# Block two of a two-block transformer kernel: norm factors applied to the products, attention woven into the following groups, the output turned per group

## The chip, the core and the metric

The kernel runs on one core of a Trainium2 chip. The metric is the device time of one execution in microseconds (us). The kernel before took 3091.04 us, the median of three runs (3089.74 to 3092.34). TensorE is called PE in the profile, VectorE DVE, ScalarE ACT, GpSimd POOL, SyncE SP.

## What is computed

Two blocks in f32 on one sequence of 256 tokens of width 2048. Block one (latent attention, short convolutions, a convolutional FFN) is not touched by the change, except that its last result now passes to block two in another way. Block two, with the last norm of block one, in the reference:

```python
x = rms_norm(x, g_final)                       # end of block one
hn = rms_norm_2(x, norm_mix_g)
z = hn @ w_in
q_a, k_a, v_a, q_b, k_b, v_b, f_logit, g_a, g_b = jnp.split(z, split_idx, axis=-1)
a = moba_attention(q_a, k_a, v_a)              # 8 heads of 128; with 256 tokens: causal, ALiBi slopes
bfx = forgetting_attention(q_b, k_b, v_b, f_logit, b_forget)   # 8 heads, causal, log-forget bias
merged = sigmoid(g_a) * (a @ w_proj_a) + sigmoid(g_b) * (bfx @ w_proj_b)
x = x + merged @ w_out
hm = rms_norm_2(x, norm_mlp_g)
x = x + square(relu(hm @ w_up)) @ w_down       # d_ff = 8192
return rms_norm_2(x, norm_final_g)
```

An rms norm multiplies each token by one number (the root factor) and each feature by a gain. The factor of a token passes through a product with weights unchanged, and through relu and square as its square.

## The kernel before

**Layout.** The activations stand turned, features on the partitions and tokens in the free dimension: `xt` holds 16 tiles (k = 0 to 15) of 128 features by 256 tokens. A product takes its weights in groups of 512 output columns. A group has 8 chunks of two k tiles (128 x 1024 f32, 512 KB); of `w_down` in block one the last groups have 6 chunks, of the projections 4. Every f32 operand of the large products is kept as two f32r parts, hi and lo, and each product is three matmuls (L1460, L1461, L1462: hi with hi, hi with lo, lo with hi), so a chunk is 24 matmuls of 128x256.

**Who does what.** SP loads raw chunks into a ring of eight (`raw`). ACT rounds a chunk to its hi part (`split`, L488), DVE subtracts to get the lo part (L818), into a ring of four (`whi`, `wlo`, NSPLIT = 4). So ACT and DVE can be four chunks ahead of PE, and split number n + 4 waits until PE has used chunk n. Each engine has its own program in a fixed order, tied to the others by semaphores. In `ahead(group, between, later)` ACT and DVE write the splits of the next group; before its fifth split stands `between`, the work on the result of the group that PE has just ended, and before its seventh `later`. PE writes groups in turn into the two halves of PSUM (`half0`, `half1`, four banks each), and `half_read` tells it that a half is free.

**Block two.** At the seam (`two_norms`, `norm_h2`) PE has ended the last `w_down` group; ACT squares `xt`, PE sums the squares over the partitions with a matrix of ones (`sums`, L1512: 16 f32 matmuls of 128x256), ACT takes the root (L532), DVE inverts (L882) and scales (L1254); the same again for `norm_mix_g_2`, whose result is split into `h2`. Then, for each branch (`alibi`, `fox`): two groups of q, two of k, two of v (token_product, L1490 to L1492), and all eight heads of attention at once, with q, k and v of eight heads in SBUF: scores (L1714, for fox with the bias matmuls L1718), maximum (L1293), exp (L634), scaling (L1106), transposes (L1725), weighted values (L1730, L1731). In the fox branch a small product FG (L1746 to L1748, 96 matmuls of 8 columns) makes the forget logits. Scores lie in the first half of PSUM and turned probabilities and results in the second, so no other group can run meanwhile. Then the eight gate groups, eight pairs of projections, `w_out`, the norm `norm_hm` (squares, sums, root, scaling, split, in one piece), four rounds of `w_up_2` and `w_down_2`, and the last norm followed by 32 transposes (L1778) to token rows, two copies (L1402) and two stores.

The line that makes attention wait for everything, and everything for attention, on PE:

```python
free(2)
attention(tag, score2(tag), turn2, weighted2)
pe.wait_ge(s_half_read, L.of("half_read", (tag, "done")))
```

Of the kernel before, what the change touches and what calls it, by code (L numbers as in the profile page):

```python
# [54 lines left out]
def constants():  # L55
# [19 lines left out]
    c["dist"] = blocks(np.where(q >= k, q - k, FAR))  # L75
    c["causal"] = blocks(np.where(q >= k, 0.0, -FAR))
# [92 lines left out]
def program(nc, ins, consts, out, known, traced):  # L169
    with ExitStack() as ctx:  # L170
# [53 lines left out]
        s_lfw = sem("lfw")  # L224

# [6 lines left out]
        def folded(h):  # L232
            return h[:, 0:2, :].rearrange("p b (s t) -> p (b s) t", s=2)

# [20 lines left out]
        eps = sb("eps", [P, 1])  # L255

# [49 lines left out]
        sc = ExitStack()  # L306
        heads2 = [sb(f"heads2_{i}", [P, HEADS, 2 * T], F32R, scope=sc) for i in range(2)]
        h2 = sb("h2", [P, KT, 2 * T], F32R, scope=sc)
        sc2 = ExitStack()
        q2 = sb("q2", [P, HEADS, T], scope=sc2)  # L310
        k2 = sb("k2", [P, HEADS, T], scope=sc2)
        v2 = sb("v2", [P, TB, HEADS * P], scope=sc2)
        dist = sb("dist_sb", [P, TB, T], scope=sc2)
        causal = sb("causal_sb", [P, TB, T], scope=sc2)
        upto = sb("upto_sb", [P, TB, T], scope=sc2)
        after = sb("after_sb", [P, TB, T], scope=sc2)
        sc2.close()
        sc2 = ExitStack()
        sigs = [sb(f"sig{i}", [P, KT, T], scope=sc2) for i in range(2)]
# [3 lines left out]
        outrow = sb("outrow", [P, TB, D], scope=sc)  # L323
        sc.close()

        p2 = sq[:, 0, :].rearrange("p (a b t) -> p a b t", a=2, b=2)
        pt2 = sq[:, 1, :].rearrange("p (a b t) -> p a b t", a=2, b=2)
        lfw = tmp[:, :, :].rearrange("p (a b) t -> p a b t", a=2)
        conv_y = [sq[:, i, :].rearrange("p (b t) -> p b t", b=4) for i in range(2)]
# [18 lines left out]
        def _(sp):  # L348
# [80 lines left out]
            groups("w_in_2", 6)  # L429

            sp.wait_ge(s_act_lo, L.of("act_lo", ("h2", KT - 1)))
            for t, n in ((dist, "dist"), (causal, "causal"), (upto, "upto"), (after, "after")):
                sp.dma_start(t[:], consts[n].rearrange("p (a t) -> p a t", a=TB)).then_inc(s_mask_in, 16)
            groups("w_in_2", 6, 3072)
            load(W["w_in_2"], 0, KT, F_AT, 8)
            with L.loop(4) as i:
                group("w_in_2", i * GW + GA_AT)
                group("w_in_2", i * GW + GB_AT)
            with L.loop(4) as i:
# [3 lines left out]
            for f in range(5):  # L443
                if f < 4:
                    groups("w_up_2", 4, f * D)
                if f > 0:
                    groups("w_down_2", 4, 0, (f - 1) * HT)
# [30 lines left out]
        def _(act):  # L478
# [322 lines left out]
            for g in range(3):  # L801
                ahead(STD, turn)
# [1011 lines left out]
```

## Time and profile before

| | us |
|---|---|
| Median of three runs | 3091.04 |
| The profiled execution, its own time | 3089.91 |
| Its span, first to last instruction | 3088.1 |
| PE busy / PE weight loads busy | 2825.3 (91%) / 2681.3 (87%) |
| DVE busy | 1823.5 (59%) |
| ACT busy | 1213.8 (39%) |
| Mean granted TensorE clock | 0.94 of full |
| Share of PE in the chain that ended last | 84% |

The share of busy time is an average over the whole program. What counts is where PE stands still, and at which clock it runs: clock 1.00 is 2.4 GHz and 0.50 is 1.2 GHz. A row of the timeline gives the start, the duration, the instruction, and in brackets how long the engine had been idle and what ended that.

### The profile page before, as it was taken

The numbers are of one execution on the slowest core, as the hardware profiler recorded it, in microseconds if no ns is written. First come the engines' busy times: TensorE is split into PE (matmuls) and PEld (weight loads), VectorE is DVE, ScalarE is ACT, GpSimd is POOL, SyncE is SP. The second block draws the span as 40 slices with busy tenths as digits, with TensorE's granted clock in tenths as the row PEclk, the third lists the DMA queues.
The fourth block names the chain that finished last, engine by engine and source line by source line (L and its number), as shares of the span: only waits on it lengthen the run. The fifth ranks groups of instructions, "written<-read, shape, count | busy, mean of one in ns | idle before, by whom it ended". The sixth has DMA issues, their size and how long they took to land.

```text
span 3088.1 us, 53349 instructions
## 1 busy us (share of the span) xinstructions
PE 2825.3 (91%) x21436; PEld 2681.3 (87%) x21436; DVE 1823.5 (59%) x2109; ACT 1213.8 (39%) x1370; POOL 17.6 (1%) x24
## 2 busy tenths in 40 slices
PE   5879977778999999999798997999899999999998
PEld 4579963468999999999795885999898999999997
DVE  3979965687666665665544443445645554555544
ACT  3733321234554453443433332444334443433332
POOL 0000000000000000000000001000000000000000
PEclk9989986789999999999998896999999999999999
DMA  5959943446655656565364450565454656566552
GB/s 176 385 165 331 327 144 95 150 160 223 198 184 177 197 185 187 160 211 178 108 186 128 130 171 28 150 181 186 163 184 131 189 185 187 187 184 187 187 185 75
DMA packets 288373, 551.55 MB, mean 179 GB/s; under 512 B 19386, under 2 KB 28328, under 8 KB 287464
## 3 DMA queue, kind: packets, MB, share of 16 engines
q1 hardware_dynamic: 286984, 547.18, 55.6%
q10 hardware_dynamic: 1248, 2.42, 0.2%
q8 instruction: 97, 1.59, 0.2%
q14 instruction: 44, 0.36, 0.0%
HBM read 547.43 MB, written 2.10 MB: 178 GB/s over the span
## 4 chain that ended last, share of the span: by engine, by line
PE 84%; DVE 10%; ACT 2%; issue 2%; DMA 1%; ACTq 1%; DVEq 0%; POOL 0%; SPq 0%
PE half L1460 24%; PE half L1461 24%; PE half L1462 24%; DVE wlo L818 3%; PE half L1512 2%; PE half L1490 1%; PE half L1491 1%; PE half L1492 1%; DVE acc L840 1%; DVE acc L837 1%; DVE tmp L1138 1%; PE half L1661 1%; PE half L1650 1%; PE half L1651 1%; PE half L1730 1%
## 5 line engine op out<-in xcount | busy, mean ns | idle before, releaser
L818 DVE TENSOR_TENSOR wlo<-raw,whi 128x1024 fp32r<-128x1024 f32 (+2 forms) x917 | 1095.9, 1209 | 891.6 <-ACT whi L488 889.9
L488 ACT ACTIVATE whi<-raw 128x1024 fp32r<-128x1024 f32 (+2 forms) x917 | 950.2, 1047 | 1277.0 <-PE half L1462 1111.2
L1460 PE MATMUL half<-hf,whi 128*128 128x256 f32 x2400 | 673.4, 281 | 10.9 <-DVE hf L891 5.1
L1461 PE MATMUL half<-hf,whi 128*128 128x256 f32 x2400 | 672.4, 280 | 0.0
L1462 PE MATMUL half<-hf,wlo 128*128 128x256 f32 x2400 | 671.4, 280 | 0.0
L1460 PE MATMUL half<-h,whi 128*128 128x256 f32 x1776 | 503.6, 284 | 37.6 <-issue 15.9
L1461 PE MATMUL half<-h,whi 128*128 128x256 f32 x1776 | 501.6, 282 | 0.0
L1462 PE MATMUL half<-h,wlo 128*128 128x256 f32 x1776 | 501.0, 282 | 0.0
L1461 PE MATMUL half<-hid,whi 128*128 128x256 f32 x1712 | 478.7, 280 | 0.0
L1462 PE MATMUL half<-hid,wlo 128*128 128x256 f32 x1712 | 478.1, 279 | 0.0
L1460 PE MATMUL half<-hid,whi 128*128 128x256 f32 x1712 | 477.9, 279 | 0.0
L1460 PEld LDWEIGHTS half<-hf,whi 128*128 128x128 f32 x2400 | 452.8, 189 | 11.9 <-issue 10.9
L1462 PEld LDWEIGHTS half<-hf,wlo 128*128 128x128 f32 x2400 | 452.1, 188 | 0.0
L1461 PEld LDWEIGHTS half<-hf,whi 128*128 128x128 f32 x2400 | 451.6, 188 | 0.0
L1460 PEld LDWEIGHTS half<-h,whi 128*128 128x128 f32 x1776 | 339.4, 191 | 39.0 <-issue 33.7
L1462 PEld LDWEIGHTS half<-h,wlo 128*128 128x128 f32 x1776 | 339.0, 191 | 0.0
L1461 PEld LDWEIGHTS half<-h,whi 128*128 128x128 f32 x1776 | 338.8, 191 | 0.0
L1460 PEld LDWEIGHTS half<-hid,whi 128*128 128x128 f32 x1712 | 321.4, 188 | 0.0
L1461 PEld LDWEIGHTS half<-hid,whi 128*128 128x128 f32 x1712 | 321.3, 188 | 0.0
L1462 PEld LDWEIGHTS half<-hid,wlo 128*128 128x128 f32 x1712 | 320.7, 187 | 0.0
L1512 PE MATMUL half<-sq,ones 128*128 128x256 f32 (+1 forms) x236 | 68.2, 457 | 38.4 <-ACT sq L526 38.4
L1460 PE MATMUL half<-mix,whi 128*128 128x256 f32 x256 | 74.6, 291 | 29.9 <-DVE tmp L1138 17.4
(216 smaller groups left out, 2863.2 us busy)
## 6 DMA issues: line engine op xcount, KB each, us to landing
raw<-in_w_up SPq DMA_DIRECT2D x288, 512.0 KB, 4.0
raw<-in_w_in SPq DMA_DIRECT2D x216, 512.0 KB, 3.8
raw<-in_w_down SPq DMA_DIRECT2D x212, 512.0 KB, 4.7
raw<-in_w_ada SPq DMA_DIRECT2D x192, 512.0 KB, 5.9
raw<-in_w_out SPq DMA_DIRECT2D x64, 512.0 KB, 4.7
raw<-in_w_proj_a SPq DMA_DIRECT2D x16, 512.0 KB, 4.5
raw<-in_w_proj_b SPq DMA_DIRECT2D x16, 512.0 KB, 4.7
raw<-in_w_up SPq DMA_DIRECT2D x16, 384.0 KB, 3.3
```

The lines of the kernel that those rows point to most:

```text
L488: A(whi[:, s, 0:elems], raw[:, c, 0:elems], ACT.Copy).then_inc(s_hi_ready, 1)
L818: V.tensor_tensor(wlo[:, s, 0:elems], raw[:, c, 0:elems], whi[:, s, 0:elems].bitcast(F32), ALU.subtract).then_inc(s_drained, 1)
L837: V.scalar_tensor_tensor(a, w[:, 0, :], s[:, 0:1], a, ALU.mult, ALU.add).then_inc(s_dve_step, 1)
L840: V.scalar_tensor_tensor(a, w[:, 1, :], s[:, 1:2], a, ALU.mult, ALU.add).then_inc(s_drained, 1)
L1138: ins_ = V.reciprocal(flat(tmp), flat(tmp))
L1460: mm(o, hi, x[:, 0:T], start=(k == 0 and b % 2 == 0), stop=False, skip_group_check=True)
L1461: mm(o, hi, x[:, T:2 * T], start=False, stop=False, skip_group_check=True)
L1462: return mm(o, lo, x[:, 0:T], start=False, stop=(k == nk - 1), skip_group_check=True)
L1490: mm(o, xh, hi, start=(k == 0), stop=False)
L1491: mm(o, xh, lo, start=False, stop=False)
L1492: ins_ = mm(o, xl, hi, start=False, stop=(k == nk - 1))
L1512: ins_ = mm(half()[:, 0, 0:width], ones[:], sq[:, j % 2, b * width:(b + 1) * width], start=(c + b == 0), stop=(c == chunks - 1 and b == pe ...
```

## The change

- **Norm factors behind the products.** `h2` and `hf` are made of `xt` with the gain alone, per group of four tiles, right behind each group that finishes these tiles (`round_x`, `lo_x`, `square_x`). The sums of squares are taken by PE one group later (`add_squares`), into an own PSUM bank. DVE turns the two norms at the seam into one factor (`roots`), and multiplies it in where q, k, v and gates leave PSUM (`times`, `values`, `gates`). For the MLP the squared factor (`root_squared`) is multiplied in behind `w_down` (`scaled_onto_x`).
- **Attention woven in.** A set `s` is now four heads: a group of q, of k, of v. The six steps of its attention are handed to PE behind chunks 1, 4 and 7 of the next two groups (`side` in `product`), to ACT and DVE at the like places of `ahead`. Scores, turned probabilities, results and sums have four PSUM banks of their own; the groups use the other four.
- **Merging.** `merged` is an own buffer, waited for per group; gates are scaled and projections gated in the instruction that leaves PSUM.
- **Output per group.** The last norm's gain is multiplied in by rows, its factor as a scale of the finished rows; squares are summed by ACT's accumulator. The transposes of groups 0 to 2 stand in the products of groups 1 to 3. Four stores take the place of two.
- The order of the groups is q, k, v, q, k, v, FG, and q, k, v twice more; loops of block two from `w_in_2` to the projections are written out.

The diff, cut to what the prediction speaks of:

```diff
+        score_bank, turn_bank, head_bank, sum_bank = [halves[i // 2][:, 2 + i % 2, :] for i in range(4)]
...
-                ahead(DN11 if g < 3 else STD, turn if g < 3 else two_norms)
+            def into_second(g):
+                turn()
+                if g == 0:
+                    act.wait_ge(s_columns, L.of("columns", "ggm"))
+                round_x("h2", g, h2, lambda k: ggm[:, k:k + 1])
+                square_x(g)
+                square_x(g, lambda k: col("g_final", k))
...
+            for s in range(4):
+                before = att[s - 1] if s > 0 else None
+                side = [{} if before is None else d for d in ({6: before}, {1: before, 4: before, 6: before}, {1: before, 4: before})]
+                ahead(STD, turn, side={2: roots()} if s == 0 else side[1])
+                ahead(STD, turn, side=side[2])
...
             for g in range(3):
-                ahead(STD, turn)
+                ahead(STD, turn, (lambda: rows(g - 1)) if g > 0 else None)
+            rows(2)
             turn()
-            squares(flat(xt))
-            root(T, rstd[:, 0:T], D)
+            rows(3)
+            act.wait_ge(s_normed, L.of("normed", "out"))
+            A(rtok[:, 2:4], rtok[:, 2:4], ACT.Sqrt).then_inc(s_root, 1)
...
+            def roots():
+                dve.wait_ge(s_summed, L.of("summed", ("sq", L.n["squared"] - 1)))
+                step(V.tensor_scalar(r1, sum_bank[:, 0:T], 1.0 / D, EPS, ALU.mult, ALU.add))
+                step(V.reciprocal(r1, r1))
+                step(V.scalar_tensor_tensor(rr, sum_bank[:, T:2 * T], 1.0 / D, r1, ALU.mult, ALU.mult))
+                step(V.tensor_scalar(rr, rr, EPS, None, ALU.add))
+                step(V.reciprocal(rr, rr))
+                tt(rr, rr, r1, ALU.mult).then_inc(s_normed, 1)
...
+            def scaled_onto_x(t, key=None):
+                times(tmp[:], r5[:])
                 dve.wait_ge(s_half_read, L.at("half_read"))
-                V.scalar_tensor_tensor(conv_y[1], conv_y[0], 0.0, conv_y[0], ALU.max, ALU.mult).then_inc(s_batch, 1)
...
+                x4 = xt[:, bass.ds(t, 4), :]
+                tt(x4, tmp[:], x4).then_inc(s_stored_x, 1)
...
                     if last:
                         ins_.then_inc(s_chunk_used, 1)
...
                         L.add("hi_ready")
+                        if side and k // KC in side:
+                            next(side[k // KC], None)
...
+            def attend(tag, s):
+                heads = range(4 * (s % 2), 4 * (s % 2) + 4)
+                pe.wait_ge(s_half_read, L.of("half_read", ("k", s)))
+                for j in range(6):
+                    if j < 4:
+                        h = heads[j]
...
+                        score2(tag, h, s).then_inc(s_scores, 1)
...
+                    if 0 < j < 5:
+                        g = heads[j - 1]
+                        for qb in range(TB):
+                            pe.wait_ge(s_probs, L.of("probs", (tag, g, qb)))
+                        turn2(g).then_inc(s_pt_turned, 1)
...
+                    if j > 1:
+                        g = heads[j - 2]
...
+                        weighted2(g).then_inc(s_heads, 1)
...
+                    yield
...
+            for s in range(4):
+                side = {} if s == 0 else {n: att[s - 1] for n in (1, 4, 7)}
+                product(of(h2), ready="h2" if s == 0 else None, side={5: add_squares(2, False, True)} if s == 0 else side)
+                product(of(h2), side={7: token_roots()} if s == 0 else side)
                 token_product(h2)
...
-            pe.wait_ge(s_act_lo, L.of("act_lo", "merged"))
-            groups(4, h2)
-            sums()
+            for g in range(4):
+                product(of(merged), ready="merged" if g == 0 else None, side={5: add_squares(1, g == 1, False)} if g > 0 else None)
...
+            for g in range(4):
+                product(of(hid[1]), side={5: turn_out(g - 1)} if g > 0 else None)
+            for _ in turn_out(3):
+                pass
```

How the instructions stand. **First place:** PE, the start of attention. Before, right behind the last v group (L1492); `half0<-k2,q2` are scores, `half1<-ident_sb,sq` transposes of probabilities, `half1<-sq,v2` the weighted values:

```order
L1492 MATMUL half0<-whi,h2 128x512
L1714 MATMUL half0<-k2,q2 128x128 [waits half_read]
L1714 MATMUL half0<-k2,q2 128x256
L1714 MATMUL half0<-k2,q2 128x128
L1714 MATMUL half0<-k2,q2 128x256
L1725 MATMUL half1<-ident_sb,sq 128x128 [waits probs] x2
L1725 MATMUL half1<-ident_sb,sq 128x128
L1730 MATMUL half1<-sq,v2 128x256 [waits pt_copied]
L1731 MATMUL half1<-sq,v2 128x128
L1714 MATMUL half0<-k2,q2 128x128
```

With the change, the third step of the first set, between the q group and the k group of the next set (L1627 to L1629 are the matmuls of a product):

```order
L1629 MATMUL half0<-h2,wlo 128x256
L1899 MATMUL half0<-k2,q2 128x128 [waits maxed]
L1899 MATMUL half0<-k2,q2 128x256
L1909 MATMUL half0<-ident_sb,sq 128x128 [waits probs]
L1909 MATMUL half0<-ident_sb,sq 128x128 x2
L1914 MATMUL half1<-sq,v2 128x256 [waits pt_copied,half_read]
L1915 MATMUL half1<-sq,v2 128x128
L1627 MATMUL half1<-h2,whi 128x256 [waits drained,half_read]
```

A head's score, the transposes of the head before it and the values of the head before that now stand together, with two or three chunks of a product between two such steps.

**Second place:** DVE, the same step. `wlo<-raw,whi` is the lo part of a weight chunk, `q2<-half0,rq` takes q out of PSUM with the factor. With the change:

```order
L909 TENSOR_TENSOR wlo<-raw,whi 128x1024 [waits hi_ready] x3
L960 TENSOR_TENSOR q2<-half0,rq 128x1024 [waits chunk_used]
L1418 SCALAR_TENSOR_TENSOR sq<-dist_sb,half0 128x384 [waits scores]
L1423 TENSOR_REDUCE stat<-sq 128x1 [waits dve_step]
L1423 TENSOR_REDUCE stat<-sq 128x1
L960 TENSOR_TENSOR heads2_0<-half1,heads2_0 128x256 [waits rounded]
L1197 RECIPROCAL stat<-stat 128x1 [waits expd]
L1201 TENSOR_SCALAR sq<-sq,stat 128x128 [waits dve_step]
L1197 RECIPROCAL stat<-stat 128x1 [waits expd]
L1201 TENSOR_SCALAR sq<-sq,stat 128x256 [waits dve_step]
L909 TENSOR_TENSOR wlo<-raw,whi 128x1024 [waits hi_ready] x2
```

Before, no `wlo` stood between the first and the last instruction of an attention; now the splits that PE needs next are queued behind each step.

## Rows read from the trace of the kernel before

**Rows 1.** Page part 2, busy tenths and granted TensorE clock in 40 slices.
```profile
PE   5879977778999999999798997999899999999998
PEclk9989986789999999999998896999999999999999
```

**Rows 2.** Timeline of PE, end of block one: start, duration, instruction, [idle before <-releaser].
```profile
1496.68 8.99 PE L1512 MATMUL half<-sq,ones 128*128 128x256 f32 x32 [5.22 <-ACT sq L526]
...
1524.62 0.58 PE L1460 MATMUL half<-h,whi 128*128 128x256 f32 x1 [4.98 <-DVE h L865]
```

**Rows 3.** Timeline of PE around the two attention stretches.
```profile
1665.22 2.90 PE L1714 MATMUL half<-k,q 128*128 128x128 f32 x8 [3.69 <-DVE v L1305]
...
1713.02 0.57 PE L1460 MATMUL half<-h,whi 128*128 128x256 f32 x1 [1.36 <-DVE stat L1300]
...
1867.10 0.35 PE L1748 MATMUL half<-whi,h 128*128 128x8 f32 x1
...
1937.45 0.58 PE L1460 MATMUL half<-h,whi 128*128 128x256 f32 x1 [1.36 <-DVE stat L1300]
```

**Rows 4.** Timeline of PE before the w_out and the w_up products.
```profile
2219.38 0.57 PE L1460 MATMUL half<-h,whi 128*128 128x256 f32 x1 [8.84 <-DVE h L865]
...
2316.97 10.14 PE L1512 MATMUL half<-sq,ones 128*128 128x256 f32 x32 [4.78 <-ACT sq L526]
...
2332.09 0.58 PE L1460 MATMUL half<-hf,whi 128*128 128x256 f32 x1 [4.98 <-DVE hf L865]
```

**Rows 5.** Chain of waits at the end: start, us, what.
```profile
3058.07 1.24 DVE xt L865
...
3081.48 2.29 DVE outrow L1402
```

**Rows 6.** Windows: us; PE, PEld, DVE, ACT, POOL busy (count); clock, DMA, GB/s.
```profile
1713.00:1721.00 8.00, 7.98 (x45) 7.99 (x46) 1.22 (x1) 1.06 (x1) 0.00 (x0) 0.63 0.01 2
1856.00:1862.00 6.00, 6.00 (x30) 6.00 (x30) 0.00 (x0) 0.00 (x0) 0.00 (x0) 0.50 0.68 228
1937.00:1941.00 4.00, 3.55 (x17) 3.56 (x18) 0.07 (x2) 0.00 (x0) 0.00 (x0) 0.53 0.00 0
2080.00:2120.00 40.00, 40.00 (x342) 40.00 (x341) 19.43 (x16) 16.27 (x16) 0.00 (x0) 1.00 0.59 185
2219.00:2227.00 8.00, 7.62 (x47) 7.63 (x48) 1.25 (x2) 1.06 (x1) 0.00 (x0) 0.68 0.01 2
2332.00:2340.00 8.00, 7.91 (x49) 7.92 (x50) 8.00 (x23) 4.60 (x11) 0.00 (x0) 0.71 0.00 0
```

**Rows 7.** Chain of waits inside the forgetting attention, at clock 0.50.
```profile
1885.37 0.85 PE half L1714 x2
...
1889.23 0.46 PE half L1725 x2
```

**Rows 8.** Line L1512, instructions of 3064 to 3068.9 us: min/median/max ns.
```profile
L1512 PE MATMUL half<-sq,ones x25: 379/379/424, 3063.6 to 3068.9; 128*128 128x256 f32 x25
```

**Rows 9.** Timeline of PE, four small f32 matmuls inside a block-one product.
```profile
702.64 0.95 PE L1431 MATMUL half<-ones,acc 128*128 128x1 f32 x8
703.45 0.36 PE L1460 MATMUL half<-mix,whi 128*128 128x256 f32 x1
```

**Rows 10.** Groups of DVE and ACT, 1600 to 3088.1 us: busy, mean ns, idle.
```profile
L818 DVE TENSOR_TENSOR wlo<-raw,whi 128x1024 fp32r<-128x1024 f32 x452 | 548.5, 1222 | 596.7 <-ACT whi L488 596.7
...
L488 ACT ACTIVATE whi<-raw 128x1024 fp32r<-128x1024 f32 x452 | 475.1, 1057 | 694.1 <-PE half L1462 621.6 <-PE half L1492 56.4 <-PE half L1748 15.2
```

**Rows 11.** Timeline of DVE, the seam: onto xt, and a reciprocal of the norm.
```profile
1493.80 1.65 DVE L1179 SCALAR_TENSOR_TENSOR xt<-half,mod_f,xt 128x256 f32<-128x256 f32 x4
...
1506.22 1.75 DVE L882 RECIPROCAL rstd<-rstd 128x256 f32<-128x256 f32 x1 [10.77 <-ACT rstd L532]
```

**Rows 12.** Timeline of ACT, a table load and its user.
```profile
1870.47 1.28 ACT L760 ACT_TABLE_LOAD   x1
1871.76 0.22 ACT L760 ACTIVATE lf<-lf 128x16 f32<-128x16 f32 x1
```

More of the change, by code:

```diff
@@ L490, in split, with ahead @@
                 L.add("drained")
-            def ahead(group, between=None, later=None, sums=0):
+            def ahead(group, between=None, later=None, sums=0, side=None):
                 L.end = L.n.get("hi_ready", 0)
@@ L505, in ahead @@
                     between()
+                if len(chunks) <= 4 and side and 4 in side:
+                    next(side[4], None)
                 if len(chunks) <= 6 and later:
@@ L842, in sum_chunks, with ahead @@
                     L.add("mod_chunks")
-            def ahead(group, between=None, later=None, sums=0):
+            def ahead(group, between=None, later=None, sums=0, side=None):
                 L.end = L.n.get("hi_ready", 0)
@@ L857, in ahead @@
                     between()
+                if len(chunks) <= 4 and side and 4 in side:
+                    next(side[4], None)
                 if len(chunks) <= 6 and later:
@@ L1375, in _ @@
-            for g in range(4):
-                ahead(STD, lambda: (onto_x(4 * g), norm_hm() if g == 3 else None))
-            def squared_relu(buf, t, key=None):
-                taken(conv_y[0])
+                lo_batch(merged, 4 * i, 4, ("merged", i))
+            for i in range(4):
+                first = i == 0
+                ahead(STD, lambda: gate(sig_a), side={1: att[3], 4: att[3], 6: att[3]} if first else None)
+                ahead(PRJ, lambda: gate(sig_b[:]), side={1: att[3], 4: att[3]} if first else None)
+                ahead(PRJ, branch_a)
+                ahead(STD, lambda: branch_b(i))
@@ L1733, in _, with add_squares @@
-            for branch, tag in enumerate(("alibi", "fox")):
-                with L.loop(2):
-                    for _ in range(2):
-                        product(of(h2), ready="h2" if branch == 0 else None)
+            def add_squares(count, first, last):
+                for i in range(count):
+                    n = L.n["squared"]
+                    pe.wait_ge(s_squared, L.of("squared", n))
+                    for b in range(4):
+                        ins_ = mm(sum_bank[:, i * T:(i + 1) * T], ones[:], sq[:, n % 2, b * T:(b + 1) * T],
+                                  start=(first and i + b == 0), stop=(last and b == 3), skip_group_check=True)
+                    ins_.then_inc(s_summed, 1)
+                    L.mark("summed", ("sq", n))
+                    L.add("squared")
+                yield
```

556 lines of the change are left out of this document (346 added, 210 removed).

## Prediction

> **What bounds the kernel now.** I read the page first: PE is busy 91% of the span and holds 84% of the chain that ended last. The 40 slices then show where it is not at its work: from the end of block one on (slice 20 of 40), PE is at 9 except in slices 20, 22, 25, 29 and 40, and the clock at 9 except in 22, 23 and 25, the two attentions [rows 1]; a gap that two slices share does not show at this grain. So DVE and ACT, at 59% and 39%, do not bound it on average; the dense stretches do, at 342 matmuls in 40 us, 0.117 us each and 2.8 us a chunk [rows 6], and the gaps between them. Next I read the timeline of PE for the edges of each gap, then the windows for the slow clock behind it. A gap costs its length, and after it the products run for some microseconds at 1.2 GHz: of 7.98 us behind the first attention, 45 matmuls are worth 45 x 0.117 = 5.3 us, so 2.7 us are lost; likewise 1.6 us behind the second, 2.1 us behind the third gap and 2.2 us behind the fourth [rows 6]. The six stretches, each with that loss:
>
> A, the seam: PE idles from 1496.68 - 5.22 = 1491.46 and the first `h2` matmul starts at 1524.62 [rows 2]: 33.2, and 1.5 for the clock (taken as behind the second attention): 34.7 us.
> B, attention alibi: from 1665.22 - 3.69 = 1661.53 to 1713.02 [rows 3]: 51.5 + 2.7 = 54.2 us.
> C, attention fox: from the end of FG at 1867.45 to 1937.45 [rows 3]: 70.0 + 1.6 = 71.6 us.
> D, waiting for the merged input: 8.8 + 2.1 = 10.9 us [rows 4, 6].
> E, the MLP norm: from 2316.97 - 4.78 = 2312.19 to 2332.09 [rows 4]: 19.9 + 2.2 = 22.1 us.
> F, the tail: from 3058.05 (DVE starts at 3058.07 [rows 5]) to the end of the span at 3088.1: 30.1 us.
> Together 223.6 us in which PE makes no product of block two. The change takes all six apart; what counts is what must be put in the dense stream instead.
>
> **What comes in their place on PE.**
> Sums of squares: 12 chunks of four f32 matmuls of 256 columns, 32 at the seam and 16 at the MLP; the last norm's 16 are gone. At full clock 25 records start within 5.3 us, 0.22 each, two to a matmul [rows 8]: 48 x 0.44 = 21.2 us.
> Attention: at clock 0.50 a score matmul of 256 columns takes 0.85 us and two transposes 0.46 [rows 7]; at full clock I take half. An alibi head has 384 columns of scores (0.64), three transposes (0.35) and 384 columns of values (0.64): 1.63 us. A fox head has 640 columns more, 2.70 us. Eight of each: 34.6 us.
> Going in and out of the product stream: four tiny f32 matmuls inside a product took 0.81 us for eight records, and behind them one start came 0.08 us late [rows 9]. For waits on several semaphores I take 0.15 us a time, for 24 attention steps and 12 other insertions: 5.4 us.
> The transposes of three of the four output groups, 24 at 0.12: 2.8 us.
> Clock behind FG: FG keeps PE busy with matmuls of 8 columns, and the clock is 0.50 in it all the same [rows 6]. FG stays as it is, so the first product behind it starts slow: 1.6 us.
> The tail F: two DVE passes of 1.22 (the factor, then the sum), eight transposes with their start 2.1, two ACT squares of 512 columns about 1.6, the last row product 0.7, small steps 0.6, the root with what is seen of its table load 0.6, two row scalings of 1.06, and from the last DVE end at 3083.77 [rows 5] to the span's end 4.3 us for the store: 14.5 us. Pieces without a row are estimates from the 1024-column rows [rows 10]. Bounds: 12 us if the two engines' halves overlap well, 18 if the four stores queue behind each other.
> Sum: 21.2 + 34.6 + 5.4 + 2.8 + 1.6 + 14.5 = 80.1 us. Gain: 223.6 - 80.1 = 143.5 us. The profiled execution took 3089.91 us, so 2946.4; it lies 1.1 below the median of the three runs, hence 2947.5, and I say **2947 us**.
>
> In the tail the root needs a table load. Here the row shows 1.28 us, and the function starts 0.01 us behind it [rows 12]; most of it lies beside DVE's last row product. The Trainium skill (ScalarE: Activation LUTs, section What ACT_TABLE_LOAD costs) has a drain of some 1.38 us on top of the 1283 ns of each switch; by it the sum would be about 2949. This trace shows the 1.28 and no drain.
>
> **What is costed at nothing, and its cover.** Each step queues on ACT and DVE ahead of the next weight splits. PE has four chunks in hand when it ends a group, 4 x 2.83 = 11.3 us. The heaviest `between` without other cover is the first seam group: ACT and DVE end split four 2.3 us after PE ended the group (L1179 started at 1493.80, PE had ended at 1491.46 [rows 2, 11]); then `onto_x` 1.65 [rows 11], four roundings, a square of 1024 and four of 256 on ACT, about 4.2, and the fifth split 1.06 + 1.22 [rows 10]: 10.4 us. It fits by 0.9 us. The later ones have PE's sums of 3.5 us as more cover. `roots` hold DVE for two reciprocals of 1.75 [rows 11] and four small passes, about 5.5 us from the end of the sums, then a root and a split, ready some 3 us before PE asks. In attention a step's results are wanted two or three chunks on (5.7 or 8.5 us, and PE's own step), and scale, maximum, exp and scaling take 6.4 to 8.6 us, the longest in the gates, where sigmoid and exp change tables; so the wait is near nothing, but not by much. POOL's bias tiles are two steps ahead. SP: the mask loads wait for a product long past, since SP is twelve chunks ahead of PE; four more loads in a stream at DMA share 0.59 [rows 6].
>
> **The rivals.**
> *Late steps.* PE waits in each of the 24 steps for a result that is just not there, as it waited 1.36 us for the last result of each attention [rows 3]. Price 24 x 1 to 1.4: 24 to 33 us, time 2971 to 2980. For it: the two-chunk distances are covered by less than 2 us. Against: four of six distances have three chunks.
> *Late splits.* The fifth chunk comes late at the norm groups and at the gates, 1 to 2 us at each of some ten places: 2957 to 2967. For it: 0.9 us of room at the first. Against: the rest has more.
> *The clock stays down in the woven stretches.* Slower than before. FG shows that the clock can be 0.50 while PE never idles, and in attention before it was mostly there [rows 1, 6, 7]. If the short f32 pieces pull it down, the eight products and the steps between them, 8 x 22.6 + 34.6 = 215 us at full clock, take twice that: 2947 + 215 = 3162. It decides the sign from 143.5/215, two thirds of that stretch at 1.2 GHz. Against: inside block one, f32 pieces within products left the spacing at 0.12 us [rows 9], and in each woven group three quarters or more of PE's time is the dense product. The Trainium skill (TensorE: Matmul & The Clock Gate, section A second HAM failure mode: psum-queue depth-cycling) tells of a kernel where short pauses between groups of matmuls were enough to make the clock swing between its two levels. No row here has such a swing inside a group.
> *The change does not do what it says.* If the first product of block two still had to wait for the whole norm, 20 us of A would stay (2967). The order of PE speaks against it: the product's waits are per two tiles.
>
> **How the numbers follow.** Forecast as costed, 2937 to 2956: 0.60. Late splits, or part of a gap left, 2956 to 2969: 0.19. Late steps, 2969 to 2985: 0.14. Clock down in part, or several of these, over 2985 but faster: 0.04. Clock down throughout: slower, 0.02. No change: 0.01. The lower end of the range is all bounds at their best: insertions at nothing (-5), tail 12 (-2.5), f32 pieces at 0.213 a record (-2): 2937. The upper end leaves out about 0.1: 2977. 0.2% of this kernel, about what a measurement can tell from no change, is 6 us. Faster 0.97, same 0.01, slower 0.02.
>
> **What would show it.** Right: PE at 9 and clock 1.00 in all slices from 20 to 39, except for FG; a first `h2` matmul within 4 us of the last `w_down` one; the two attentions gone as stretches, with records of L1899 at 0.2 us a piece between products; `w_out` and `w_up` starting at once; from the last product matmul to the end some 14 us. Per step: idle of PE before L1909 and L1914 under 0.3 us. Wrong: waits of L1909 on DVE of a microsecond each (late steps), of L1627 on L909 (late splits), or a granted clock under 0.9 in windows of the woven groups. A tail over 18 us would mean the stores.

## The result, and the profile after

The changed kernel takes 2873.62 us (median of four runs, 2871.43 to 2890.53) against 3091.69 us (four runs, 3089.74 to 3092.99): a ratio of 0.9307, 95% interval 0.9271 to 0.9343. The gain is 218 us; 143.5 us were forecast, and the time lies 63 us below the range's lower end. The profiled execution took 2872.42 us.

First the profile page of the changed kernel, the engines' busy time and the 40 slices of PE and its clock, which answer to [rows 1]:

```profile
span 2870.6 us, 52211 instructions
PE 2684.6 (94%) x21408; PEld 2571.9 (90%) x21408; DVE 1794.6 (63%) x2056; ACT 1224.7 (43%) x1407; POOL 20.8 (1%) x24
...
PE   4959977768899999999999999999999999999998
...
PEclk9989987769999999999999899999999999999999
```

From the 21st slice on PE is at 9 until the tail, and the clock has one slice below 9, at FG. Then the waits of PE from 1480 us to the end:

```profile
engine line waited for: us in total, times, longest us
PE half L2004 <- DVE xt L960: 2.6, 1, 2.6
```

In all of block two PE waits once, for the last transposes of the output. So no step of attention and no split comes late, and the stretches A to E are gone: what was forecast of the mechanisms holds. The timeline of PE shows what stands in their place, one set of sums behind a chunk and one step of the forgetting attention (start, duration, instruction):

```profile
1491.20 3.61 PE L1883 MATMUL half<-sq,ones 128*128 128x256 f32 x16
```
```profile
1743.32 0.28 PE L1629 MATMUL half<-h,wlo 128*128 128x256 f32 x1
1743.44 0.38 PE L1899 MATMUL half<-k,q 128*128 128x128 f32 x2
1743.66 0.39 PE L1903 MATMUL half<-after_sb,tmp 128*128 128x128 f32 x2
1743.88 0.60 PE L1899 MATMUL half<-k,q 128*128 128x256 f32 x2
1744.32 1.03 PE L1903 MATMUL half<-after_sb,tmp 128*128 128x256 f32 x4
1745.18 0.49 PE L1909 MATMUL half<-ident_sb,sq 128*128 128x128 f32 x3
1745.51 0.60 PE L1914 MATMUL half<-sq,v 128*128 128x256 f32 x2
1745.94 0.38 PE L1915 MATMUL half<-sq,v 128*128 128x128 f32 x2
1746.08 0.36 PE L1627 MATMUL half<-h,whi 128*128 128x256 f32 x1
```

No row has a bracket: PE goes from a product into the step and out of it without idling, 2.76 us from the last product matmul's start to the next one's.

The surprise stands in windows that the prediction did not compare, because nothing in them was changed. Windows of 60 us, before (the columns are those of [rows 6]); the first lies in block one:

```profile
900.00:960.00 60.00, 60.00 (x511) 60.00 (x511) 42.58 (x52) 33.76 (x39) 0.00 (x0) 1.00 0.56 171
2500.00:2560.00 60.00, 60.00 (x512) 60.00 (x511) 32.50 (x28) 23.65 (x23) 0.00 (x0) 1.00 0.60 191
```

and after:

```profile
900.00:960.00 60.00, 60.00 (x532) 60.00 (x531) 41.79 (x47) 30.62 (x36) 0.00 (x0) 1.00 0.65 205
2500.00:2560.00 60.00, 60.00 (x532) 60.00 (x532) 33.92 (x29) 25.25 (x24) 0.00 (x0) 1.00 0.59 194
```

PE is full and the granted clock 1.00 in all four, yet 532 product matmuls stand where 511 or 512 did. Such a count includes the two or three matmuls that only reach into the window, so it serves to compare; the *spacing*, the time from the start of one product matmul to the start of the next, is read from the starts. Every third matmul of a product has the same line. Before, and then after, with number, duration and first and last start between 2500 and 2560 us:

```profile
L1460 PE MATMUL half<-hid,whi x127: 279/279/279, 2515.2 to 2559.7; 128*128 128x256 f32 x127
```
```profile
L1627 PE MATMUL half<-hid,whi x165: 276/276/276, 2504.1 to 2559.9; 128*128 128x256 f32 x165
```

That is 44.5 us for 126 x 3 matmuls, 0.1177 us each, and 55.8 us for 164 x 3, 0.1134 us each; to one more digit the starts are 117.8 and 113.3 ns apart. Up to the first sum of squares, which the changed kernel has at 1433 us, block one's instructions on PE are the same in both kernels. Both traces have 19,632 such matmuls, so up to 19,632 x 4.5 ns = 88 us hang on this.

What does differ in block one is where tiles stand in SBUF. The changed kernel allocates five small tiles (`ggm`, `rq`, `r5`, `rtok`, `square_sum`: 64 + 1024 + 1024 + 32 + 32 = 2176 bytes per partition, each start at a multiple of 32) between `eps` and the big scopes. Every operand that moves through PE in a product (`h1`, `hctx`, `qn`, `kvn`, `mix`, `hf`, `hid`, `h2`, `heads2`) starts 2176 bytes later, and the new `merged` lies in line with them, while the split weights `whi` and `wlo` stay. I call *distance* the start of `hf` less the start of `whi`, modulo 256 bytes. The tiles between add up to 56,896 bytes before, distance 64, and 59,072 after, distance 192; the other moving tiles and `wlo` lie multiples of 256 bytes from these.

### The profile page after: what moved, and what is told of

Read it like the earlier page. It is cut to its first block, busy times and chain, and to the rows that moved or that the text cites. A ratio compares the mean times of both kernels' runs of the same rounds, so it can differ in the third digit from the quotient of the medians.

```text
span 2870.6 us, 52211 instructions
## 1 busy us (share of the span) xinstructions
PE 2684.6 (94%) x21408; PEld 2571.9 (90%) x21408; DVE 1794.6 (63%) x2056; ACT 1224.7 (43%) x1407; POOL 20.8 (1%) x24
## 4 chain that ended last, share of the span: by engine, by line
PE 86%; DVE 9%; issue 2%; ACT 2%; DMA 1%; ACTq 1%; DVEq 0%; SPq 0%
PE half L1627 25%; PE half L1629 25%; PE half L1628 25%; DVE wlo L909 2%; PE half L1683 1%; DVE acc L931 1%; PE half L1661 1%; PE half L1663 1%; DVE acc L928 1%; PE half L1662 1%; DVE tmp L1233 1%; DMA raw<-in_w_ada 1%; PE half L1832 1%; PE half L1821 1%; PE half L1822 1%
## 5 line engine op out<-in xcount | busy, mean ns | idle before, releaser
L1627 PE MATMUL half<-hf,whi 128*128 128x256 f32 x2400 | 663.9, 277 | 6.2 <-DVE hf L986 5.1
L1628 PE MATMUL half<-hf,whi 128*128 128x256 f32 x2400 | 663.4, 276 | 0.0
L1629 PE MATMUL half<-hf,wlo 128*128 128x256 f32 x2400 | 663.4, 276 | 0.0
L1627 PE MATMUL half<-hid,whi 128*128 128x256 f32 x1712 | 474.0, 277 | 0.0
L1629 PE MATMUL half<-hid,wlo 128*128 128x256 f32 x1712 | 473.4, 276 | 0.0
L1627 PEld LDWEIGHTS half<-hf,whi 128*128 128x128 f32 x2400 | 451.4, 188 | 7.0 <-issue 5.5
L1629 PEld LDWEIGHTS half<-hf,wlo 128*128 128x128 f32 x2400 | 451.3, 188 | 0.0
L1627 PE MATMUL half<-h,whi 128*128 128x256 f32 x1520 | 430.5, 283 | 21.1 <-issue 15.9
L1628 PE MATMUL half<-h,whi 128*128 128x256 f32 x1520 | 426.7, 281 | 0.0
L1629 PE MATMUL half<-h,wlo 128*128 128x256 f32 x1520 | 426.5, 281 | 0.0
L1627 PEld LDWEIGHTS half<-hid,whi 128*128 128x128 f32 x1712 | 321.6, 188 | 0.1
L1629 PEld LDWEIGHTS half<-hid,wlo 128*128 128x128 f32 x1712 | 321.6, 188 | 0.0
L1627 PEld LDWEIGHTS half<-h,whi 128*128 128x128 f32 x1520 | 289.9, 191 | 21.6 <-issue 15.9
L1628 PEld LDWEIGHTS half<-h,whi 128*128 128x128 f32 x1520 | 290.6, 191 | 0.3
L1629 PEld LDWEIGHTS half<-h,wlo 128*128 128x128 f32 x1520 | 290.8, 191 | 0.0
L1627 PE MATMUL half<-mix,whi 128*128 128x256 f32 x256 | 74.0, 289 | 30.2 <-DVE tmp L1233 17.4
L931 DVE SCALAR_TENSOR_TENSOR acc<-raw,silu_sb,acc 128x512 f32<-128x512 f32 x128 | 96.2, 752 | 4.5
```

The lines of the kernel that those rows point to most:

```text
L931: V.scalar_tensor_tensor(a, w[:, 1, :], s[:, 1:2], a, ALU.mult, ALU.add).then_inc(s_drained, 1)
L1627: mm(o, hi, x[:, 0:T], start=(k == 0 and b % 2 == 0), stop=False, skip_group_check=True)
L1628: mm(o, hi, x[:, T:2 * T], start=False, stop=False, skip_group_check=True)
L1629: return mm(o, lo, x[:, 0:T], start=False, stop=(k == nk - 1), skip_group_check=True)
```

## The experiments

Unless the text says otherwise, an edit is made to the changed kernel. Ratios are to the kernel before, run again beside the experiments: median 3088.93 us beside e1 to e4, 3088.36 beside e5 to e8, 3089.22 beside e9 to e12 and 3090.29 beside e13 to e16.

### Moving the tiles, and moving the code

**e1**, the kernel before with 2176 more bytes behind `eps`:

```diff
         eps = sb("eps", [P, 1])
+        pad = sb("pad", [P, 544])
```

> The kernel before with 2176 unused bytes per partition behind eps, so that every tile allocated after it (hf, hid, h, mix and the others that the product matmuls read) starts 2176 bytes later, as in the changed kernel; no instruction differs. In the trace of before the product matmuls start 0.1176 us apart in every stretch (x511 in 60 us), in that of after 0.1133 us apart in most (x532), in block one too, whose instructions are the same. Theory P (placement): the spacing follows the address, so x530 or so in 60 us here, and 19,500 products at up to 4.3 ns less give 3008 to 3025 us. Theory I (the instruction stream, or how the program stands in memory): x511 and 3091 us. Theory R (rhythm: the spacing is set by how a product starts after its waits): some stretches at each spacing, 3010 to 3091 us.

3022.01 us (3009.11 to 3041.94), ratio to before 0.9782, interval 0.9728 to 0.9836. Without one changed instruction the old kernel gains 67 us, the time of theory P. Its profiled execution (3031.33 us) has both spacings, one after the other; the change comes at 1313 us:

```profile
900.00:960.00 60.00, 60.00 (x512) 60.00 (x511) 42.07 (x49) 31.73 (x35) 0.00 (x0) 1.00 0.58 181
2500.00:2560.00 60.00, 60.00 (x532) 60.00 (x531) 30.36 (x25) 23.55 (x23) 0.00 (x0) 1.00 0.64 193
```

Some stretches at each spacing is what theory R has, so placement is not all.

**e2**, the changed kernel with its tiles moved on to the old place modulo 1024 bytes:

```diff
         square_sum = sb("square_sum", [P, TB, 4])
+        pad = sb("pad", [P, 224])
```

> The changed kernel with another 896 unused bytes behind its five new small tiles, so that the tiles behind them stand 3072 bytes later than in before, at the same place within 1024 bytes. Theory P with a period of up to 1024 bytes: x511 in 60 us and about 2945 us. Theories I and R: as the changed kernel, 2873 us or near it.

2942.40 us (2935.49 to 2943.72), ratio 0.9522, interval 0.9502 to 0.9542. The whole change, at the old distance, is worth 146.5 us (3088.93 - 2942.40); 143.5 were forecast. The spacing is back everywhere, as in this window:

```profile
2500.00:2560.00 60.00, 60.00 (x511) 60.00 (x511) 30.94 (x26) 26.00 (x25) 0.00 (x0) 1.00 0.61 189
```

e1 and e2 fill the square: the placement gives 67 us to the old code and 69 us (2942.40 - 2873.62) to the new one, so the two gains add. The 67 us are a median over runs that differ by 33 us, so that the two agree this closely is in part luck.

**e3**, the kernel before with 64 bytes (distance 128):

```diff
         eps = sb("eps", [P, 1])
+        pad = sb("pad", [P, 16])
```

> The kernel before with 64 unused bytes per partition behind eps: all tiles behind start at multiples of 128 bytes instead of 64 beyond one. Theory P, if the place within 128 bytes matters: a spacing that differs from 0.1176 us in every stretch. Theories I and R: 3091 us.

3109.38 us, ratio 1.0063 (1.0042 to 1.0084): 20 us slower than before, with 502 matmuls in the window 2500 to 2560 us, a spacing of 120.0 ns. Placement can also cost.

**e4**, the kernel before with one transpose done twice, no tile moved:

```diff
                 for k in range(KT):
+                    if tb + k == 0:
+                        nc.tensor.transpose(half()[:, 0, 0:P], stage[:, 0, 0:P], ident[:])
```

> The kernel before with one transpose of the first token tile done twice, so that all of TensorE's instructions behind it stand one weight load and one matmul later; no tile moves. Theory I: spacings change in some stretches, 3010 to 3090 us. Theories P and R: 3091 us, x511 in 60 us.

3085.07 us, ratio 0.9994 (0.9982 to 1.0006): no change. But the profiled execution (3081.8 us of span) has a stretch, from 1318 to 1484 us, in which the old placement runs at the fast spacing:

```profile
900.00:960.00 60.00, 60.00 (x512) 60.00 (x511) 42.91 (x52) 33.18 (x39) 0.00 (x0) 1.00 0.55 169
1400.00:1460.00 60.00, 60.00 (x532) 60.00 (x532) 33.25 (x40) 23.57 (x23) 0.00 (x0) 1.00 0.60 188
```

PE's timeline has the place where it changes, a wait inside block one that the kernel before has too:

```profile
1316.92 0.28 PE L1462 MATMUL half<-hf,wlo 128*128 128x256 f32 x1
1317.99 0.38 PE L1460 MATMUL half<-hf,whi 128*128 128x256 f32 x1 [0.79 <-DVE wlo L818]
```

The stretch alone would fit theory I, but e1 to e3 move the time with no instruction changed, and here the median stays. So the distance does not fix one spacing. It makes one likely; within a run the stream can change from one to the other. The kernel before may do it at times as well: beside e9 to e12, two of its seven runs took 3064.49 and 3070.44 us, the others 3087.64 to 3091.07, but no trace shows these two.

### Distance or absolute place

**e7**, 128 bytes behind the small tiles (distance 64, at another place modulo 512 than in before):

```diff
+        pad = sb("pad", [P, 32])                  # behind square_sum
```

> The changed kernel with 128 unused bytes behind its five small tiles, so that hf, hid, h, merged start at 192 beyond a multiple of 256 bytes, as in before and in e2_after_back, but not at their place within 512 or 1024 bytes. Placement with a period of 256 bytes: x511 in 60 us, 2942 us. Placement with a period of 512 or more: another spacing. Rhythm alone (a product's start decides): near 2873 us.

2940.25 us (2921.10 to 2943.14): as e2. So a place modulo 512 or 1024 bytes is not what counts.

**e8**, the same 128 bytes, but ahead of `whi`, so that the weights move along (distance 192):

```diff
+        pad = sb("pad", [P, 32])
         whi = sb("whi", [P, NSPLIT, CW], F32R)
```

> The changed kernel with 128 unused bytes ahead of whi: the split weights and every tile behind them stand 128 bytes later, so hf, hid, h, merged are at 192 beyond a multiple of 256 as in e7_pad128, and whi and wlo move along with them. If the place of the moving operand alone counts: as e7_pad128. If its place against the weights counts: as the changed kernel, x532 in 60 us and 2873 us.

2878.34 us (five runs, 2869.90 to 2895.88): as the changed kernel. e7 and e8 have the moving tiles at the same addresses; only the weights, and the small tiles between them and the moving ones, stand 128 bytes apart, and that is worth 62 us. The profiled execution is the slowest of the five: 512 matmuls from 900 to 960 us, 532 from 2500 to 2560 us, so distance 192 has the slow spacing in part of it.

**e13**, 128 bytes ahead of `whi` and 128 behind the small tiles: the moving tiles at their own place modulo 256, distance 64.

```diff
+        pad = sb("pad", [P, 32])
         whi = sb("whi", [P, NSPLIT, CW], F32R)
...
+        pad2 = sb("pad2", [P, 32])                # behind square_sum
```

> The changed kernel with 128 unused bytes ahead of whi and 128 more behind the small tiles: whi and wlo stand 128 bytes later, the moving tiles 256 bytes later, so these are at their own place modulo 256 and their distance from the weights is 64 instead of 192. Theory D (the distance of weights and moving tiles modulo 256 bytes decides): 118 ns a product and 2940 us, as e2 and e7. Theory A (the place of the moving tile, and in e8 something else): 2873 us.

2943.16 us (2917.12 to 2948.60): as e2. The small tiles stand here as in e8, so it is not their place that made e8 fast.

**e14**, 64 bytes ahead of `whi` (`sb("pad", [P, 16])`): everything moves, distance 192.

> The changed kernel with 64 unused bytes ahead of whi: weights and moving tiles 64 bytes later, distance 192 as before the shift. Theory D: as the changed kernel, 2870 to 2880 us. Theory A or any dependence on the weights' own place modulo 128: 2930 us or more.

2876.21 us (2872.82 to 2879.24). With e7, e8 and e13 the cross is complete: three placements at distance 64 take 2940 to 2943 us, three at 192 take 2874 to 2878 us, wherever the tiles themselves stand.

**e15**, 128 bytes between `whi` and `wlo`: distance 64 from `whi`, 192 from `wlo`.

```diff
         whi = sb("whi", [P, NSPLIT, CW], F32R)
+        pad = sb("pad", [P, 32])
         wlo = sb("wlo", [P, NSPLIT, CW], F32R)
```

> The changed kernel with 128 unused bytes between whi and wlo: whi unmoved, wlo and the moving tiles 128 bytes later. Distance from whi (two of three matmuls) 64, from wlo (the third) 192. Theory D, matmul by matmul: two thirds of the way from 2873 to 2941, 2918 us. If one poor distance among the three spoils the rhythm of all: 2940 us.

2915.87 us (2888.11 to 2918.41), the time that theory D gave, yet not in the way it meant. The windows show no mean of two spacings: block one and most of block two up to the projections are slower than either (507 matmuls, also from 1900 to 1960 us), and from `w_out` on nearly all is at the fast one:

```profile
900.00:960.00 60.00, 60.00 (x507) 60.00 (x506) 42.48 (x52) 32.71 (x38) 0.00 (x0) 1.00 0.56 174
...
2500.00:2560.00 60.00, 60.00 (x532) 60.00 (x531) 33.78 (x28) 29.07 (x29) 0.00 (x0) 1.00 0.61 192
```

That the median fell on the forecast is chance; "matmul by matmul" is refuted.

### The other distances

**e9, e10, e11, e12, e16**: 32, 64, 96, 224 and 160 bytes behind the small tiles, as in e7.

> The changed kernel with 32 unused bytes behind its five small tiles. The distance of the moving tiles (h, hf, hid, merged) from the split weights, modulo 256 bytes, was 64 in before, e2 and e7 (118 ns a product, 2940 to 2942 us for the changed kernel), 128 in e3 (118 to 119.5 ns), 192 in the changed kernel, e1 and e8 (113.3 ns in most stretches, 2873 to 2878 us). Here it is 224. Theory S (the best place is one of a smooth course over the distance, with its worst near 96 to 128 and its best opposite it): as the changed kernel or a little better, 2865 to 2880 us. Theory M (the placement only matters in steps of 64 bytes): as one of its neighbours, 2873 us or that of distance 0.

> The same with 64 unused bytes: distance 0 modulo 256. Theory S: 2865 to 2900 us. Rival, same place for both operands is the worst case (each read of weights meets a read of the moving tile): above 2942 us.

> The same with 96 unused bytes: distance 32 modulo 256. Theory S: between the spacings of 0 and 64, 2900 to 2942 us. Theory M: as distance 0 or as distance 64 (2942 us).

> The same with 224 unused bytes: distance 160 modulo 256. Theory S: between the spacings of 128 and 192, 2890 to 2945 us. Theory M: as distance 128 (about 2960 us) or as distance 192 (2873 us).

> The changed kernel with 160 unused bytes behind its small tiles: distance 96 modulo 256, the last step of 32 that was not tried. The medians so far by distance are 0: 2983, 32: 2932, 64: 2941, 160: 2949, 192: 2874, 224: 2954 us. No smooth course; 64 is below 160 and 224, 192 alone is much below. Expected 2940 to 2960 us; a second good place (under 2900 us) would show as a rival that the good places lie 96 or 128 apart.

The changed kernel by distance (change of padding alone), with the matmuls in 60 us of block one (900 to 960 us) and of block two (2500 to 2560 us):

| distance | run | median us | matmuls, block one | matmuls, block two |
|---|---|---|---|---|
| 0 | e10 | 2983.14 | 502 | 502 |
| 32 | e11 | 2932.48 | 517 | 512 |
| 64 | e2 | 2942.40 | 512 | 511 |
| 96 | e16 | 2982.33 | 503 | 503 |
| 160 | e12 | 2948.93 | 514 | 508 |
| 192 | the change | 2873.62 | 532 | 532 |
| 224 | e9 | 2953.57 | 509 | 509 |

Distance 128 has only the kernel before (e3). From best to worst it is 109.5 us, 3.8%. Theory S, a smooth course, is refuted: 224 was to be as good as 192 and is 80 us worse, and 0 is the worst; that e11 fell into its range does not save it. Theory M is too: 224 equals neither 192 nor 0, and 160 (e12) is neither at 2873 nor at 2960 us. The rival recorded with e10, that the same place for both operands is the worst case, forecast the time of distance 0 rightly; but 96, where 2940 to 2960 us were expected, takes the same 2982 us without that coincidence, so it explains nothing here. No other good place was found, and with it fell e16's rival of a second one. Of the seven distances tried the changed kernel stands by chance on the best; the kernel before stands at the one that is third of the seven for the changed kernel.

### Taking the change apart, at the old distance

**e5**, the kernel of e2 with the six steps of each set's attention in one piece:

```diff
+def whole(steps):
+    for _ in steps:
+        pass
+    yield
...
-            att = [attend("alibi" if s < 2 else "fox", s) for s in range(4)]
+            att = [whole(attend("alibi" if s < 2 else "fox", s)) for s in range(4)]
```

(on PE, ACT and DVE alike).

> The kernel of e2_after_back (changed kernel, tiles placed as before; 2942.4 us) with all six steps of each set's attention in one piece behind chunk 1 of the next group, on PE, ACT and DVE. By the prediction's terms weaving saves B and C (125.8 us) less the 34.6 of their matmuls and 24 insertions of 0.15 us: 88 us, so 3030 us; with two more fills of the pipeline of heads and two more slow starts up to 3046. A rival: the buffer of four chunks and the own PSUM banks hide part of it, under 3000 us. Another: the gain of the change came from the placement alone and weaving gives little: under 2965 us.

2988.38 us (2975.58 to 2992.05), 46 us over e2: not the 88 of the prediction's terms, and not next to nothing either; the time lies where the first rival put it, under 3000 us, part of the gap being hidden. PE's waits and its timeline at the end of the last set:

```profile
PE half L1916 <- DVE sq L1208: 13.4, 7, 2.4
PE half L1906 <- DVE stat L1430: 13.2, 10, 2.9
PE half L1921 <- DVE heads L967: 4.1, 4, 1.0
```
```profile
1878.09 0.38 PE L1922 MATMUL half<-sq,v 128*128 128x128 f32 x2
1880.87 0.87 PE L1916 MATMUL half<-ident_sb,sq 128*128 128x128 f32 x3 [2.40 <-DVE sq L1208]
...
1884.05 1.19 PE L1921 MATMUL half<-sq,v 128*128 128x256 f32 x2 [1.02 <-DVE heads L967]
...
1885.32 0.56 PE L1634 MATMUL half<-h,whi 128*128 128x256 f32 x1
```

The last set occupies 1864.76 to 1885.32 = 20.6 us; all four take 20.0, 19.8, 20.4 and 20.6 us, together 81 us for 16 heads. In before the 16 heads took 51.5 + 70.0 = 121.5 us. So 41 us of what B and C lost went with the way one head runs, and only the 46 us with the weaving. Windows of before over the fox attention, and of e5 over half of it:

```profile
1867.50:1937.40 69.90, 45.95 (x136) 32.89 (x136) 24.18 (x78) 20.02 (x54) 14.58 (x16) 0.62 0.03 8
```
```profile
1864.80:1885.30 20.50, 13.89 (x71) 11.20 (x70) 10.95 (x32) 7.54 (x24) 4.08 (x4) 0.88 0.19 54
```

Over all heads PE is busy 76.4 of 121.3 us before, at a granted clock of 0.59 and 0.62, and 49.6 of 80.5 us in e5, at 0.76 to 0.90. So some 27 of the 41 us are busy time and 14 us are waits. Busy time times clock is nearly the same, some 46 and 42 us (an estimate: the clock is a mean over busy and idle time alike), so the 27 us are mostly the clock. That the shorter waits come from the own PSUM banks and from one instruction over a head's 384 score columns is argued, not tried. The prediction's sum is untouched by it, since it subtracted what stands in the stream at the end; that weaving alone saves 88 us, as e5's expectation has it, was wrong.

**e6**, the kernel of e2 with the first products of `h2`, `merged` and `hf` waiting for the whole operand:

```diff
                         n = min(k0 + KC, nk) - 1
+                        n = KT - 1 if ready in ("h2", "hm", "merged") else n
```

> The kernel of e2_after_back with the first product of h2, of merged and of hf in block two waiting for the last tile of its operand instead of for the two that it reads. In the trace of e2_after_back the last part of merged is done 7.8 us and that of hf 5.5 us after their first product starts. With some 9 us for h2 and 1.6 to 2.7 us at the slow clock behind each wait: 2942 + 22 + 6 = 2970 us, 2964 to 2978. If the waits by pairs of tiles hide nothing (rival: the splits are late anyway): 2942 to 2948 us.

2962.79 us (2959.91 to 2965.19), 20.4 us over e2. Idle time before the first matmul of each, from PE's timeline:

```profile
1507.60 0.36 PE L1629 MATMUL half<-h,whi 128*128 128x256 f32 x1 [2.95 <-issue]
...
2114.90 0.55 PE L1629 MATMUL half<-merged,whi 128*128 128x256 f32 x1 [7.60 <-issue]
...
2219.50 0.55 PE L1629 MATMUL half<-hf,whi 128*128 128x256 f32 x1 [5.96 <-issue]
```

16.5 us of waiting; most of the rest is the slow clock behind the two longer waits (0.62 and 0.75 in the 8 us from their ends; 1.00 behind the first). The time is 1 us under the expected range. `merged` and `hf` wait as expected; `h2` waits 3 us and not 9, because its rounding is done sooner after the last group of block one than I had worked out.

## Why the prediction was wrong, point by point

**The step that failed** stands in its first paragraph: dense stretches "at 342 matmuls in 40 us, 0.117 us each". It was read well enough (by starts it is 0.1178), and then carried unsaid into the changed kernel as if it belonged to the instruction. It belongs to the placement of its operands too. After, product matmuls start 113.3 ns apart in most stretches, and the 69 us between e2 and the changed kernel are this alone: both have the same 21,408 matmuls on PE in the same order, and of the 69.1 us between the spans of the two traces, 68.3 lie between one product matmul and the next. No rival named it; the range could not hold it, since its lower end was "all bounds at their best" of the costs inside block two, while some 26 us of the gain fall in block one. (In e2 the sums behind the last `w_down` chunk of block one end at 1500.3 us, in the changed kernel at 1474.1.)

**At the old distance the sum was right.** e2's profiled execution took 2941.5 us, against 2946.4 forecast, 5 us off. Term by term, from the trace of e2, each from the start of the last product matmul before a piece to the start of the next behind it (3.38 us for a first sum of squares, say), less one spacing of 0.12 a piece:

| term | forecast | measured | from |
|---|---|---|---|
| sums of squares | 21.2 | 19.2 | 4 x (3.38 - 0.12) and 4 x (1.66 - 0.12) |
| attention | 34.6 | 32.4 | 2 x 6.6 (alibi) and 2 x 11.0 (fox), less 24 x 0.12 |
| in and out of the stream | 5.4 | 4.3 | late starts behind 36 pieces, see below |
| transposes | 2.8 | 2.4 | 3 x (0.91 - 0.12) |
| roots turned per token | none | 0.4 | 4 matmuls of one column |
| clock behind FG | 1.6 | 2.8 | 28 spacings in 6.1 us, at 0.118 each 3.3 |
| tail | 14.5 | 14.4 | 2856.2 to 2870.6 in the changed kernel |

Together 75.9 us against 80.1 forecast. For in and out of the stream, the starts right behind a piece of attention in e2:

```profile
1597.78 0.36 PE L1628 MATMUL half<-h,whi 128*128 128x256 f32 x1
1597.99 0.28 PE L1629 MATMUL half<-h,whi 128*128 128x256 f32 x1
1598.11 0.28 PE L1630 MATMUL half<-h,wlo 128*128 128x256 f32 x1
```

The second product matmul comes 0.21 us behind the first, 0.09 late, and the third on time. So it is behind all 36 pieces: 0.08 to 0.09 us late, 0.19 behind the sums of squares and the first step of a set. The picture of [rows 9], one start late behind each piece, was right, and the allowance of 0.15 us a time a little high.

**A, D, E** (gaps at the norms and the merged input) closed: no PE wait in the trace, and the first `h2` matmul starts 3.4 us behind the last `w_down` one. e6 gives the part of that which is the waiting by pairs of tiles, 20 us; that the rest comes from having no norm between the products any more is what is left over, not a run of its own. The 0.9 us of room at the first seam group was enough.

**B and C** closed. Each of the 24 steps runs without an idle bracket, so the rival *late steps* fell; so did *late splits*.

**F**: the tail's chain in the changed kernel, against [rows 5]:

```profile
2856.19 1.24 DVE tmp L960
2857.45 1.24 DVE xt L960
2858.73 1.11 PE half L2004 x8
2859.86 1.27 ACT sq L880 x4
2861.14 1.28 ACT L890
2862.44 0.21 ACT rtok L890
2862.67 0.18 DVE rtok L1563
2862.87 1.15 ACT outrow L895
2864.02 1.04 ACTq L171
```

14.4 us, forecast 14.5, though pieces differ: the transposes take 1.1 and not 2.1, the squares 1.3 and not 1.6; the table load stands in the chain in full, which I had put mostly beside other work, and the end, from 2864.02 us on, takes 6.6 us, where the second row scaling and 4.3 us behind it, 5.4 us together, were put. The load takes 1.28 us and the root starts 0.02 us behind it. The drain of 1.38 us that the Trainium skill (ScalarE: Activation LUTs, section What ACT_TABLE_LOAD costs) puts on top does not show here either.

**The clock stays down in the woven stretches**: fell. The granted clock is 1.00 in windows over the woven groups, for example in the kernel of e2 over a set of alibi and one of fox:

```profile
1577.00:1607.00 30.00, 30.00 (x248) 29.54 (x248) 21.26 (x40) 15.46 (x28) 0.00 (x0) 1.00 0.53 167
1822.00:1850.00 28.00, 28.00 (x225) 27.39 (x224) 16.76 (x27) 12.89 (x19) 4.54 (x4) 1.00 0.53 157
```

Where the same steps stand in one piece (e5), with PE waiting between them, it falls:

```profile
1579.90:1610.00 30.10, 21.44 (x117) 18.45 (x116) 15.15 (x39) 11.21 (x28) 0.00 (x0) 0.77 0.17 51
```

Woven into the products and without a wait, the short f32 pieces leave the clock at 1.00. Whether it falls in e5 for the waits or for the missing products between the pieces, these runs don't separate.

## What to carry to other kernels

A change that adds or removes a small tile moves every tile allocated behind it, and here that alone moved the time by 67 us of 3089 with no instruction changed. Before a gain is credited to the code, put the tiles back with padding and time both; and where PE is bound by a dense stream of short matmuls, try the few placements of the moving operand against the weights as a change of its own. A spacing read from the trace belongs to instruction, placement and stretch together: compare it in a stretch that the change does not touch before explaining anything else.

## What the runs showed of the hardware

With PE full and clock 1.00, a pair of weight load and matmul of 256 moving columns starts every 113.3 ns (the changed kernel) to 120.0 ns (e10), depending on where the operands stand against each other. The Trainium skill (TensorE: Matmul & The Clock Gate, section Wait — 56ns, not 53.3ns?) gives, for matmuls back to back, columns through 2.4 GHz plus some 2.5 ns, by which an estimate for 256 columns is 109 ns. The trace, with a weight load to each, has 113.3 ns at best; that section's figures have no term for placement, and here the measurement decides.

In windows of 60 us three counts recur in several runs (532, 511 or 512, 502 or 503: 113.3, 117.8 and 120.0 ns), with 507 to 517 at some distances. A spacing holds for tens to hundreds of microseconds and can change within one execution: the fast one was seen at distance 64 (e4), the slow one at 192 (in e1, in block one of e8, and in the changed kernel between 310 and 369 us). In the traces of the changed kernel, e1, e4, e8 and e14 the stream goes over from 113.3 to 117.8 ns, or back, only where something interrupts it: a wait, a piece of other matmuls, or (twice in e8) a product matmul that starts 0.1 us or more late. Between two interruptions it keeps its spacing, but for a few matmuls. Which of the two comes behind an interruption is at some places the same from trace to trace. In the changed kernel the stream is at 117.8 ns between the sums of squares of `w_out`, and at 113.3 behind the last of them, which ends at 2172 us:

```profile
2124.00:2145.00 21.00, 21.00 (x180) 21.00 (x180) 10.78 (x13) 9.86 (x12) 0.00 (x0) 1.00 0.56 175
2175.00:2196.00 21.00, 21.00 (x188) 21.00 (x187) 13.54 (x12) 10.36 (x10) 0.00 (x0) 1.00 0.62 176
```

e8 and e14, also at distance 192, have 180 or 181 and 188 matmuls at the same two places. That a stretch can have either spacing fits that runs of one kernel spread: 3009 to 3042 us in e1, where both were seen, and 2982 to 2984 in e10, where the windows have 502 or 503 throughout.

**What stays open.** That the distance between moving tiles and weights decides which spacings come, and how often, the runs show (e7, e8, e13, e14). Why, they don't: whether the reads of the weights and of the moving tile meet in SBUF, which of the spacings a stream takes up behind an interruption, and why 192 is good and 224 is not. Steps under 32 bytes, distance 128 for the changed kernel, tiles placed one by one (but for `wlo` in e15), and the old distance restored in only one block were not tried. No version was found that is faster than the changed kernel.
